# Four query levels of the next HGRN chunk padded by ScalarE at the end of the chunk before, with the last round written out

## The reference

```
xn = RMSNorm(h); u = xn @ w_in                     # 1024 -> 6144 columns
f  = lb + (1 - lb) * sigmoid(hf)
S_t = diag(f_t) S_{t-1} + (1 - f_t) i_t^T          # HGRN2, 8 heads, state 64x64
o_t = S_t^T silu(hq_t)
retention: 4 heads of 128, rotary q and k, decay gamma_h
per-head RMSNorm and swish gate of both, mixed by sigmoid gates, w_out, residual
ConvFFN (w_up, causal width 3, gelu * gate, w_down), residual
h += sigmoid(RMSNorm(h) @ w_ple_gate) * (p @ w_ple); final RMSNorm
```

## Time and profile before

| | us |
|---|---|
| median of three runs | 967.33 |
| the profiled execution | 967.89 |
| its span in the profile | 966.1 |
| TensorE busy | 938.3 (97%) |
| VectorE busy | 531.1 (55%) |
| ScalarE busy | 394.6 (41%) |
| GpSimd busy | 238.7 (25%) |

### The profile page before, as it was taken

One profiled execution on the slowest core, in us unless ns is written; L12 is line 12 of the kernel. 1 busy time (PEld: TensorE's weight loads), 2 busy tenths in 40 slices (PEclk: granted clock), 3 DMA queues, 4 the chain that ended last, 5 costly groups with the idle time before them and its releaser, 6 DMA issues.

```text
span 966.1 us, 20940 instructions
## 1 busy us (share of the span) xinstructions
PE 938.3 (97%) x7834; PEld 916.1 (95%) x7834; DVE 531.1 (55%) x632; ACT 394.6 (41%) x524; POOL 238.7 (25%) x280
## 2 busy tenths in 40 slices
PE   6999999999999999999999999999999999999995
PEld 6999998998999999899999999999999999999994
DVE  5322267677656545566566555666566343435453
ACT  5432355455445445423334444444443222222433
POOL 0007066756411011000551111111111031212331
PEclk9999999999999999999999999999999999999997
DMA  7133522212233233354232322223323433322202
GB/s 238 50 101 91 175 71 72 76 54 66 65 99 93 85 105 109 102 177 121 88 88 72 103 88 87 87 87 97 98 87 95 121 90 90 90 87 82 82 29 94
DMA packets 168053, 91.49 MB, mean 95 GB/s; under 512 B 13585, under 2 KB 166561, under 8 KB 167601
## 3 DMA queue, kind: packets, MB, share of 16 engines
q1 hardware_dynamic: 149698, 80.61, 28.1%
q10 hardware_dynamic: 18320, 10.42, 3.8%
HBM read 83.10 MB, written 8.00 MB: 94 GB/s over the span
## 4 chain that ended last, share of the span: by engine, by line
PE 94%; ACT 2%; DVE 1%; issue 1%; DMA 1%; ACTq 0%; SPq 0%; DVEq 0%
PE acc L476 82%; PE lvb L554 3%; DMA xtok<-in_x_prompt 1%; PE lvb L666 1%; PE mb L678 1%; ACT zq L889 1%; PE lvb L517 1%; PE ob L603 0%; PE mb L590 0%; ACT L941 0%; PE ob L656 0%; PE mb L660 0%; PE ob L598 0%; PE lvb L637 0%; PE ob L655 0%
## 5 line engine op out<-in xcount | busy, mean ns | idle before, releaser
L1118 DVE TENSOR_TENSOR wlo<-raw,whi 128x1024 fp32r<-128x1024 f32 (+2 forms) x132 | 193.0, 1463 | 179.0 <-ACT whi L798 179.0
L798 ACT ACTIVATE whi<-raw 128x1024 fp32r<-128x1024 f32 (+2 forms) x132 | 146.5, 1111 | 352.5 <-PE acc L476 351.4
L476 PE MATMUL acc<-xah,whi 128*128 128x260 f32 x896 | 186.9, 290 | 0.0
L476 PE MATMUL acc<-xah,wlo 128*128 128x260 f32 x896 | 180.3, 283 | 0.0
L476 PE MATMUL acc<-xal,whi 128*128 128x260 f32 x896 | 179.9, 282 | 0.0
L476 PE MATMUL acc<-xbh,whi 128*128 128x260 f32 x832 | 168.6, 284 | 3.2 <-DVE tg L1475 2.4
L476 PE MATMUL acc<-xbh,wlo 128*128 128x260 f32 x832 | 167.7, 283 | 0.0
L476 PE MATMUL acc<-xbl,whi 128*128 128x260 f32 x832 | 167.4, 283 | 0.0
L476 PEld LDWEIGHTS acc<-xah,whi 128*128 128x128 f32 x896 | 137.9, 189 | 9.0 <-issue 8.2
L476 PEld LDWEIGHTS acc<-xah,wlo 128*128 128x128 f32 x896 | 137.9, 188 | 0.0
L476 PEld LDWEIGHTS acc<-xal,whi 128*128 128x128 f32 x896 | 137.8, 188 | 0.0
(11 more groups left out here) (285 smaller groups left out, 1230.2 us busy)
## 6 DMA issues: line engine op xcount, KB each, us to landing
raw<-in_w_in SPq DMA_DIRECT2D x96, 256.0 KB, 3.1
raw<-in_w_up SPq DMA_DIRECT2D x88, 256.0 KB, 3.1
raw<-in_w_down SPq DMA_DIRECT2D x16, 384.0 KB, 3.2
raw<-in_w_down SPq DMA_DIRECT2D x16, 320.0 KB, 3.7
raw<-in_w_out SPq DMA_DIRECT2D x16, 256.0 KB, 3.0
raw<-in_w_ple_gate SPq DMA_DIRECT2D x8, 512.0 KB, 3.7
x_transposed<-xstg SPq DMA_DIRECT2D x1, 2080.0 KB, 7.6
hT<-x_transposed ACTq DMA_DIRECT2D x1, 2080.0 KB, 9.8
```

What stands on the lines that cost most here:

```text
L476: mm = pe.matmul(acc[tile % 2][:, b, 0:HT], wt[slot][:, w], xx[:, c, b * HT:(b + 1) * HT], start=first and i == 0 and q == 0, stop=last an ...
L798: act.activation(whi[k % 2][:, 0:n], raw[k % 2][:, 0:n], ACT.Copy).then_inc(hi_ready, 1)
L1118: dve.tensor_tensor(wlo[k % 2][:, 0:n], raw[k % 2][:, 0:n], whi[k % 2][:, 0:n].bitcast(fp), SUB).then_inc(lo_ready, 1)
```

## The change

ScalarE's four rounds become three rounds of a loop and a fourth that is written out. The pads of levels 0 to 3 leave the head of the round: those of round 0 stand ahead of the loop, those of round `it+1` stand in round `it` behind the copy `v8r` and ahead of the wait for unit 3. The written-out round has no such pads. Nothing changes on the other engines.

```diff
-            with act.Fori(0, 4) as it:
-                for l in range(4):
-                    pad_queries(l, it)
+            for l in range(4):
+                pad_queries(l, 0)
+
+            def hgrn_chunk(it, last=False):
                 act.wait_ge(misc_full, it * 6 + (M_B - 2))
...
                 done("B", 2, it)
-                ahead("B", 2, it)
+                ahead("B", 2, it, "C" if last else None)
...
                 act.activation(v8r[:, bass.ds(it * 128, 128)], lvb[0:NS, 1, 0:128], ACT.Copy).then_inc(v_taken, 1)
+                if not last:
+                    for l in range(4):
+                        pad_queries(l, it + 1)
                 done("B", 3, it)
-                ahead("B", 3, it)
+                ahead("B", 3, it, "C" if last else None)
                 act.activation(two(sg[1][:]), ps2(3), ACT.Sigmoid).then_inc(sig_ready, 1)
                 branch_hi(ahh, it, 0)
+
+            with act.Fori(0, 3) as it:
+                hgrn_chunk(it)
+            hgrn_chunk(3, last=True)
```

## The result

The changed kernel takes 979.31 us (median of four runs, 977.89 to 980.22) against 967.00 us before (four runs on the same chip). The ratio is 1.0123, with a 95% interval of 1.0107 to 1.0139. It is slower, as forecast, but by 12.3 us and not by 3.4, outside the range of 968.9 to 972.4. The profiled execution took 979.77 us with a span of 978.0, which is 11.9 more than the span before.

A forecast was written before the change was run, and what follows sets the result against it. TensorE, busy 97% of the span, bounds the kernel; at each of three passages late merges delay the second scores by 1.14 us, so 967.33 + 3.4 = 970.8 us. The 8-in-10 range is 968.9 to 972.4.

The forecast's parts named there:

- two chains of equal length meet at `scores(1)`: At TensorE's second scores, the chains through pads and merges end together; shortening the pads' alone yields under 0.15 us.
- the waits for `zq` go: At the three passages between section B's rounds, TensorE no longer waits 1.3 us each for ScalarE's pads.
- waits for the merges take their place: Three TensorE pauses of about 2.4 us before the second scores, released by VectorE's merges.
- the pads' 3.9 us: TensorE's waits for pads at three passages; rival that all are gained, 963.4 us, chance 0.05.
- ScalarE's spill: Moved pads overrun ScalarE's idle gap before unit 3 by 1.42 us; sigmoid 1.42 late, `grt` on VectorE 1.17 late.
- VectorE's idle time before `grt`: Sign of the forecast: VectorE idles some 0.7 us before `grt`, released by ScalarE's sigmoid.
- the forecast's pause: TensorE's pause at each passage, growing from 1.27 to 2.4 us and standing before the second scores.
- Queued behind it ... `vblk` and the preparation of levels 4 and up. All come 1.17 us late: Behind `grt`, VectorE's work through both merges and GpSimd's `vblk` and later levels all shift by 1.17 us.
- one pair of instructions in each other's way, `fs` and `vblk`: VectorE's copy `fs` waits out GpSimd's `vblk`; both move together, so `fs` still takes 1.87 us.
- I charge nothing for the clock: TensorE's longer pauses cost no clock: it stayed at 1.00 in 888 to 894 us, with 1.98 us without a matmul.
- The written-out round and the table loads: ScalarE's new code costs nothing, 0.8 us at most; rival of extra table load or code pause, chance 0.07.
- the 3 x 1.14: The whole forecast loss: second scores 1.14 us later at each of three passages, +3.4 us.

The follow-up runs named there:

- two-level kernels: Pads of levels 0 and 1 moved, 2 and 3 left behind `branch_hi`: 977.01 us; also GpSimd's level 4 held back: 967.48; or sample copies between `merge(0)` and `merge(1)`: 962.95.
- e4: Changed kernel with 20 unused matmuls on TensorE between unit 0 and the second scores in rounds 1 to 3: 973.31 us, ratio 1.0071.
- e10: Changed kernel with VectorE's sample copies between `merge(0)` and `merge(1)`: 966.63 us, ratio 0.9990.
- e1: Kernel before with only the loop form (three rounds and a written-out fourth), pads still behind `branch_hi`: 966.63 us, ratio 1.0001.
- e7: Kernel before with VectorE's sample copies put behind the merges of all four levels, pads unchanged: 978.51 us, ratio 1.0106.
- e8: Changed kernel with only the pads of levels 0 and 1 moved and GpSimd's level 4 held back until the sample copies are done: 967.48 us, ratio 0.9996.
- e11: Kernel before with VectorE's sample copies between `merge(0)` and `merge(1)`, pads unchanged: 968.77 us, ratio 1.0005.
- e3: Changed kernel with VectorE's sample copies put behind the merges of all four levels: 977.70 us, ratio 1.0102.
- e5: Changed kernel with only the pads of levels 0 and 1 moved and VectorE's sample copies behind the merges of all four levels: 979.12 us, ratio 1.0109.
- e6: Changed kernel with GpSimd's level 4 held back until VectorE's sample copies are done: 971.82 us, ratio 1.0061.
- e2: Changed kernel with only the pads of levels 0 and 1 moved, levels 2 and 3 left behind `branch_hi`: 977.01 us, ratio 1.0102.

## Why the prediction was half right

- That two chains of equal length meet at `scores(1)`, that the waits for `zq` go and that waits for the merges take their place: right, and the core of it. The two-level kernels show that the pads' 3.9 us can be had only when the merges move too.
- ScalarE's spill: forecast 1.42 us, `grt` 1.17 us late; measured 1.23. VectorE's idle time before `grt` is 0.82 us, forecast 0.7. The kernel with level 4 held back has the forecast's pause, 2.5 against 2.4 us.
- "Queued behind it ... `vblk` and the preparation of levels 4 and up. All come 1.17 us late": this step failed first. Level 4 needs the first scores and `vblk`. Before the change the scores came last (203.71, 0.25 us behind the end of `vblk`), when VectorE's copy `fs` had got through. With the scores 1.27 us sooner and `vblk` later, GpSimd goes from one to the other without a gap (level 4 starts 0.95 us late, not 1.17), and the copies of level 4 take the place of `vblk` in VectorE's way: 0.6 us more at each of two passages, 1.2 in all. Why the third is spared stays open. I counted on one pair of instructions in each other's way, `fs` and `vblk`, and not on the next. The Trainium skill (SBUF — State Buffer, section "Who interferes with whom") states that of VectorE in a two-port mode and GpSimd, whichever issues first has the shared pair for the whole instruction. The trace agrees on the whole instruction, `fs` ending at 209.35, 0.03 us behind the end of `lq` at 209.32. It does not bear out the order: by the recorded starts `fs` (207.14) was there 1.79 us before `lq` (208.93), and `lq` went ahead of it.
- "I charge nothing for the clock": this step failed by most, 6.0 us in section B. Its row showed a clock of 1.00 in one pause, and I took that one case for a rule. The pause is one of 2.37 us, of which the row has 1.8: it ends at 894.00, 0.6 us before TensorE goes on, so it could not show what comes behind the pause. The clock stayed up there in that execution, but the same place in the changed kernel has the same pause and a lower clock behind it, 1.5 us. One case where something didn't happen was no bound. The two ends should have been 0 and the loss of half the clock for some us; with the 7.5 us measured here, the range would have reached to 979.
- The written-out round and the table loads: nothing, as charged. The count of loads is the same, four each at the root and the sigmoid.
- Sum: forecast 3.4. Between the two profiled executions it was merges 4.9, clock in section B 6.0, clock late 1.5, less 0.5: 11.9. That the change costs time was forecast for the right reason; but of the 12.3 us only the 3 x 1.14 were in the forecast.

## What to carry to other kernels

When a wait on the bound engine is to be removed, look for the second wait at its next meeting point and measure its slack; here it was under 0.2 us, and both chains had to be shortened at once. Releasing work earlier also releases its other users: list every engine that waits for the same event and what each will then run beside. And a longer pause of TensorE is to be charged twice, with its length and, as the upper end, with a slower stretch behind it, if it comes to the lengths that had one (1.7 us and more here).

## What the runs showed of the clock

At a pause of TensorE in section B the granted clock fell to half for 3.4 us (once 6.8, at the first passage of the changed kernel), or stayed at 1.00. It fell in the last part of the pause or, at the three passages, within 1.1 us behind it. Over the profiles of this case, by the length of the pause at the three passages:

| pause, us | places | clock fell |
|---|---|---|
| 0.29 to 0.92 | 6 (e4, e10) | 0 |
| 1.26 to 1.33 | 15 (before, e1, e7, e8, e11) | 0 |
| 1.69 to 2.10 | 9 (e3, e5, e7) | 5 |
| 2.48 to 2.49 | 3 (e6) | 2 |
| 2.55 to 3.19 | 6 (changed kernel, e2) | 6 |

In the changed kernel TensorE had worked for over 30 us without a wait ahead of each of its three falls. The pause late in the kernel (892.24 to 894.61 us before the change, 2.37 to 2.41 us in all 13 profiles) had a fall behind it in 8 profiles and none in 5, of kernels that differ only in section B. What decides between a fall and none at one length was not tried.
